# The halves of a weight chunk word by word in one buffer: a two-layer fp32 network on one core

## The reference

```python
def _conv_ffn(h, w_in, conv_w, conv_b, w_out):
    u = h @ w_in                                   # 2048 -> 2 x 5632
    ...
    return (jax.nn.silu(gate) * val) @ w_out       # 5632 -> 2048

for i in range(DEPTH):
    a = _rmsnorm(h, norm_mix[i])
    ...                                            # y: latent or windowed attention
    h = h + y
    h = h + _conv_ffn(_rmsnorm(h, norm_ffn[i]), ...)
return _rmsnorm(h, final_norm)
```

## Time and profile before

| | us |
|---|---|
| median of 2 runs | 1994.73 |
| lowest, highest | 1994.3, 1995.16 |
| span of the profiled execution | 1992.6 |
| PE busy in it | 1979.7 (99%) |
| DVE, ACT, POOL busy | 1418.9 (71%), 992.0 (50%), 143.9 (7%) |

### The profile page before, as it was taken

The page is one execution under the profiler, slowest core; times in us unless marked ns, Lnnn a source line. Parts: engine busy times, 40 slices in busy tenths (PEclk is TensorE's granted clock), DMA queues, the critical chain, the costliest instruction groups (busy, mean ns, idle before and its releaser), DMA issues.

```text
span 1992.6 us, 33224 instructions
## 1 busy us (share of the span) xinstructions
PE 1979.7 (99%) x11726; PEld 1746.3 (88%) x11726; DVE 1418.9 (71%) x1969; ACT 992.0 (50%) x1180; POOL 143.9 (7%) x157
## 2 busy tenths in 40 slices
PE   9999999999999999999999999999999999999998
PEld 8998888888888888888899899888888888888886
DVE  6856788877887786554567668788778877865444
ACT  6556445555545554343455654554555555534433
POOL 1112220000000000110120004100000000011000
PEclk9999999999999999999999999999999999999999
DMA  8566655555555555556575445655555556676654
GB/s 299 177 196 161 196 188 189 177 200 191 189 175 193 193 194 192 190 176 205 191 237 179 132 136 179 197 184 178 190 193 195 189 183 196 207 235 213 200 188 137
DMA packets 106870, 379.67 MB, mean 191 GB/s; under 512 B 12107, under 2 KB 12684, under 8 KB 106668
## 3 DMA queue, kind: packets, MB, share of 16 engines
q1 hardware_dynamic: 102332, 362.22, 54.7%
q0 software_dynamic: 4176, 16.07, 3.2%
q10 hardware_dynamic: 288, 0.33, 0.1%
HBM read 368.09 MB, written 10.49 MB: 190 GB/s over the span
## 4 chain that ended last, share of the span: by engine, by line
PE 96%; DVE 2%; DMA 1%; SPq 0%; ACT 0%; issue 0%; ACTq 0%
PE ps L429 46%; PE ps L432 24%; PE ps L823 4%; PE ps L822 4%; PE ps L821 4%; PE ps L723 2%; PE ps L725 2%; PE ps L724 2%; DMA raw<-weights 1%; DVE w_lo L1172 1%; PE ps L761 1%; PE ps L784 1%; PE ps L459 1%; PE ps L460 1%; PE ps L458 1%; PE ps L772 1%
## 5 line engine op out<-in xcount | busy, mean ns | idle before, releaser
L1172 DVE TENSOR_TENSOR w_lo<-raw,w_hi 128x1024 fp32r<-128x1024 f32 (+1 forms) x678 | 824.9, 1230 | 498.5 <-ACT w_hi L861 477.2
L861 ACT ACTIVATE w_hi<-raw 128x1024 fp32r<-128x1024 f32 (+1 forms) x678 | 710.4, 1054 | 778.4 <-PE ps L432 454.9
L429 PE MATMUL ps<-op_in,w_hi 128*128 128x512 f32 x2992 | 1026.4, 391 | 1.7 <-DVE w_lo L1205 0.9
L432 PE MATMUL ps<-op_in,w_lo 128*128 128x256 f32 x2992 | 812.3, 282 | 0.0
L429 PEld LDWEIGHTS ps<-op_in,w_hi 128*128 128x128 f32 x2992 | 548.9, 188 | 106.1 <-issue 1.3
L432 PEld LDWEIGHTS ps<-op_in,w_lo 128*128 128x128 f32 x2992 | 564.8, 189 | 15.7
L429 PE MATMUL ps<-op_ffn,w_hi 128*128 128x512 f32 x704 | 243.1, 390 | 0.0
L432 PE MATMUL ps<-op_ffn,w_lo 128*128 128x256 f32 x704 | 195.8, 282 | 0.0
L429 PEld LDWEIGHTS ps<-op_ffn,w_hi 128*128 128x128 f32 x704 | 131.1, 188 | 26.5
L821 PE MATMUL ps<-w_hi,op_ffn 128*128 128x512 f32 x352 | 139.5, 396 | 0.0
L822 PE MATMUL ps<-w_lo,op_ffn 128*128 128x512 f32 x352 | 139.5, 396 | 0.0
(11 more groups left out here) (218 smaller groups left out, 2052.4 us busy)
## 6 DMA issues: line engine op xcount, KB each, us to landing
raw<-weights SPq DMA_DIRECT2D x662, 512.0 KB, 4.1
raw<-weights SPq DMA_DIRECT2D x16, 384.0 KB, 3.1
bias_rows<-brow POOLq DMA_DIRECT2D x1, 6144.0 KB, 36.1
win_bias<-bias_rows POOLq DMA_DIRECT2D x4, 1024.0 KB, 8.4
h<-xt SPq DMA_DIRECT2D x8, 256.0 KB, 7.2
raw<-weights SPq DMA_DIRECT2D x8, 256.0 KB, 6.2
x_tok<-x_rows SPq DMA_DIRECT2D x4, 512.0 KB, 8.7
h_rows<-h_blocks POOLq DMA_DIRECT2D x16, 128.0 KB, 5.5
```

Source lines behind the costliest of these rows:

```text
L429: return mm(ps[:, bank, 0:2 * T], whi, op, start=start, stop=stop)
L432: return mm(ps[:, bank, 0:T], wlo, op[:, 0, :], start=False, stop=False)
L861: f(w_hi[s][:, 0:cols], raw[s][:, 0:cols], ACT.Copy).then_inc(hi_ready, 1)
L1172: v.tensor_tensor(w_lo[s][:, 0:cols], raw[s][:, 0:cols], w_hi[s][:, 0:cols].bitcast(F32), ALU.subtract).then_inc(lo_ready, 1)
```

## The change

`w_hi[s]` and `w_lo[s]` are no buffers of their own any more. A slot of the ring is one buffer of 2048 words; in it a chunk's high and low half lie in one of two ways, by how PE will use the chunk:

- word by word (`w_hi`, `w_lo`: even and odd words), where all its tiles are stationary: a_in, a_q, a_out, f0_in, f0_out, the last 32 chunks of b_in, b_out, f1_in;
- one behind the other as before (`rows_hi`, `rows_lo`: first and last 1024 words), where a chunk or part of it moves: a_kv, the first 8 chunks of b_in, f1_out.

ACT and DVE write with the same choice, and DVE reads the high half with it. Since the layout is fixed when the program is built, loops are split where it changes: ACT's and DVE's loops over a_kv, over f0_out (unrolled: 88 chunks) and the last turn of f1_in. Number, size and order of matmuls, splits, loads and waits stay the same.

```diff
-    w_hi = [new(f"w_hi{s}", [P, CH], F32R) for s in range(SLOTS)]
-    w_lo = [new(f"w_lo{s}", [P, CH], F32R) for s in range(SLOTS)]
+    ring = [new(f"ring{s}", [P, 2 * CH], F32R) for s in range(SLOTS)]
+    w_hi = [r[:, :].rearrange("p (c two) -> p c two", two=2)[:, :, 0] for r in ring]
+    w_lo = [r[:, :].rearrange("p (c two) -> p c two", two=2)[:, :, 1] for r in ring]
+    rows_hi = [r[:, 0:CH] for r in ring]
+    rows_lo = [r[:, CH:2 * CH] for r in ring]
...
-            def w_chunk(n, op, kt0, first, last, b0, tiles=(0, 1, 2, 3)):
+            def w_chunk(n, op, kt0, first, last, b0, tiles=(0, 1, 2, 3), halves=(w_hi, w_lo)):
                 s = n.mod(SLOTS)
+                whi, wlo = halves[0][s], halves[1][s]
                 pe.wait_ge(lo_ready, (n + 1).v)
                 for j, m in enumerate(tiles):
                     for k in range(2):
                         c = k * COLS + m * P
-                        z = feature_tile(b0 + j, w_hi[s][:, c:c + P], w_lo[s][:, c:c + P],
+                        z = feature_tile(b0 + j, whi[:, c:c + P], wlo[:, c:c + P],
                                          op[:, kt0 + k, :, :], first and k == 0, last and k == 1)
...
-                        mm(o, hi, wcols(w_hi[s], k), start=first and k == 0, stop=False)
-                        mm(o, hi, wcols(w_lo[s], k), start=False, stop=False)
-                        z = mm(o, lo, wcols(w_hi[s], k), start=False, stop=last and k == 1)
+                        mm(o, hi, wcols(rows_hi[s], k), start=first and k == 0, stop=False)
+                        mm(o, hi, wcols(rows_lo[s], k), start=False, stop=False)
+                        z = mm(o, lo, wcols(rows_hi[s], k), start=False, stop=last and k == 1)
...
-            def split(n, cols=CH):
+            def split(n, cols=CH, hi=w_hi):
...
-                f(w_hi[s][:, 0:cols], raw[s][:, 0:cols], ACT.Copy).then_inc(hi_ready, 1)
+                f(hi[s][:, 0:cols], raw[s][:, 0:cols], ACT.Copy).then_inc(hi_ready, 1)
...
-            def split(n, cols=CH):
+            def split(n, cols=CH, halves=(w_hi, w_lo)):
...
-                v.tensor_tensor(w_lo[s][:, 0:cols], raw[s][:, 0:cols], w_hi[s][:, 0:cols].bitcast(F32),
+                v.tensor_tensor(halves[1][s][:, 0:cols], raw[s][:, 0:cols], halves[0][s][:, 0:cols].bitcast(F32),
                                 ALU.subtract).then_inc(lo_ready, 1)
...
-                repeat(act, 0, FFN_TURNS, body)
+                repeat(act, 0, FFN_TURNS - layer, body)
+                if layer == 1:
+                    body(None, FFN_TURNS - 1)
...
-            residual(PH["f0_out"], FT, OP0["f0_out"])
+            residual(PH["f0_out"], FT, OP0["f0_out"], rows_next=True)
```

More of the change, by code:

```diff
@@ L820, in rows_half @@
                     hi, lo = op_ffn[1][:, kt0 + k, 0, t], op_ffn[1][:, kt0 + k, 1, t]
-                    mm(ps[:, bank + half, :], hi, w_hi[s][:, w], start=first and k == 0, stop=False)
-                    mm(ps[:, bank + half, :], hi, w_lo[s][:, w], start=False, stop=False)
-                    z = mm(ps[:, bank + half, :], lo, w_hi[s][:, w], start=False, stop=last and k == 1)
+                    mm(ps[:, bank + half, :], hi, rows_hi[s][:, w], start=first and k == 0, stop=False)
+                    mm(ps[:, bank + half, :], hi, rows_lo[s][:, w], start=False, stop=False)
+                    z = mm(ps[:, bank + half, :], lo, rows_hi[s][:, w], start=False, stop=last and k == 1)
                 return z
@@ L954, in q_group @@
                 for c in range(2):
-                    split(k.times(2) + (ph.c0 + AHEAD_2 + c), cols)
+                    split(k.times(2) + (ph.c0 + AHEAD_2 + c), cols, w_hi if cols < CH else rows_hi)
                     if c == 0 and k.c == 5:
@@ L974, in kv_group @@
                     for c in range(2):
-                        split(k.times(2) + (ph.c0 + AHEAD_2 + c))
-            repeat(act, 0, 3, lambda i: [kv_group(Lin(k, 2, i)) for k in range(2)])
-            kv_group(Lin(6))
+                        split(k.times(2) + (ph.c0 + AHEAD_2 + c), hi=rows_hi if k.c < 5 else w_hi)
+            repeat(act, 0, 2, lambda i: [kv_group(Lin(k, 2, i)) for k in range(2)])
+            for k in range(4, 7):
+                kv_group(Lin(k))
             kv_group(Lin(7), False)
@@ L1033, in body @@
                     for j in range(2 * per):
-                        split(Lin(ph.c0 + AHEAD + j + 2 * per * t, 2 * per, i))
+                        next_rows = rows_next and t == 1 and j >= 2 * per - AHEAD
+                        split(Lin(ph.c0 + AHEAD + j + 2 * per * t, 2 * per, i), hi=rows_hi if next_rows else w_hi)
                         gi, at = divmod(j, per)
@@ L1037, in body @@
                             op_high(Lin(k0 + gi + 2 * t, 2, i), op_in[:, sl(Lin(4 * gi + 8 * t, 8, i), 4), 0, :])
-                if second:
+                if rows_next:
+                    body(None, 0)
+                if second or rows_next:
                     body(None, 1)
@@ L1141, in _ @@
                 for c in range(FT // 2):
-                    split(Lin(ph.c0 + AHEAD + FT // 2 * g + c))
+                    split(Lin(ph.c0 + AHEAD + FT // 2 * g + c), hi=rows_hi)
                     if c == 19:
@@ L1356, in q_group @@
                         rope_finish(Lin(8), 3, xr[:, 1, :], q_rope[:, UNITS_A - 1:UNITS_A, :])
-                    split(k.times(2) + (ph.c0 + AHEAD_2 + c), cols)
+                    split(k.times(2) + (ph.c0 + AHEAD_2 + c), cols, (w_hi, w_lo) if cols < CH else (rows_hi, rows_lo))
             for k in range(UNITS_A):
@@ L1375, in kv_group @@
                     for c in range(2):
-                        split(k.times(2) + (ph.c0 + AHEAD_2 + c))
-            repeat(dve, 0, 3, lambda i: [kv_group(Lin(k, 2, i)) for k in range(2)])
-            kv_group(Lin(6))
+                        split(k.times(2) + (ph.c0 + AHEAD_2 + c), halves=(rows_hi, rows_lo) if k.c < 5 else (w_hi, w_lo))
+            repeat(dve, 0, 2, lambda i: [kv_group(Lin(k, 2, i)) for k in range(2)])
+            for k in range(4, 7):
+                kv_group(Lin(k))
             kv_group(Lin(7), False)
@@ L1459, in add_residual, with residual @@
                 dve.wait_ge(banks_free, (g + 1).v)
-            def residual(ph, kts, k0, gain, bias=None, second=False):
+            def residual(ph, kts, k0, gain, bias=None, second=False, rows_next=False):
                 per = kts // 2
@@ L1466, in body @@
                     for j in range(2 * per):
-                        split(Lin(ph.c0 + AHEAD + j + 2 * per * t, 2 * per, i))
+                        next_rows = rows_next and t == 1 and j >= 2 * per - AHEAD
+                        split(Lin(ph.c0 + AHEAD + j + 2 * per * t, 2 * per, i),
+                              halves=(rows_hi, rows_lo) if next_rows else (w_hi, w_lo))
                         gi, at = divmod(j, per)
```

44 lines of the change are left out of this document (24 added, 20 removed).

## The result

The changed kernel takes 2024.73 us against 1994.73 us: 1.0151 times as long, 95% interval 1.0126 to 1.0175. It is 30 us slower, 1.5%, where 80 us less had been forecast. The interval does not reach 1.

What follows compares the result with a forecast made beforehand. PE, busy 99% of the span, was taken as the bound. Pairs (70.8 us) and narrow matmuls (8.9 us) were to save 79.7 us, splits and loops nothing: 1994.7 - 79.7 = 1915 us, range 1886 to 2078 us.

Steps and rivals of the forecast that it cites:

- What bounds the kernel: PE, busy 99% of the span: time is the number of matmuls times the step from start to start.
- The excess over the columns: F32R matmuls in feature_tile: 26.7 ns a pair and 10.0 ns a narrow matmul over their columns, put down to colliding streams.
- With a step of 8 bytes the load advances as fast as an F32R operand moves: Stepped weight loads on PE: distance between load and moving operand stays constant; at best 106 us less in all.
- three quarters of the gain: Changed pairs and narrow matmuls on PE: 17.5 ns less a pair, 6.2 a narrow one, 79.7 us in all.
- The place matters: Wide matmuls in f0_out and f1_out, same size and clock, different operands: 3.8 ns apart, so excess is no fixed price.
- Loads get slower: Rival, PE's weight loads: a tile spread over 1024 bytes doubles the excess, 106 us more, 2101 us; chance 0.11.
- The splits: ACT's copy (1059 ns) and DVE's subtraction (1232 ns) of 1024 columns keep their length with a step of two words.
- DVE's 0.57 us of room a split: In f0_in, with 176 splits, each split may grow by 0.57 us before DVE is full.
- DVE becomes the bound: Rival, f0_in and f1_in: splits grow to 2.1 us, 2080 us in all, break-even at 1.86 us; chance 0.15.
- The excess is F32R's own: Rival, F32R matmuls on PE: excess is a price of F32R itself, the step changes nothing, 1995 us; chance 0.16.
- The signs to look for: Right if f0_out pairs step by about 329 ns, narrow matmuls 110, f1_out's 234, splits 1232 and 1059, f0_in about 465 us.
- the first step: The claimed PE gain from stepped weight tiles; wrong if pairs still step by 347 ns or above.

Runs made afterwards that it cites:

- m3_columns: Kernel of its own, 24 matmuls a line averaged over eight places, varying tile size, step, moving columns and type; F32R with 512 columns 231 ns, BF16 216.
- m2_places: Kernel of its own, 16 pairs a line in feature_tile's order at 16 activation starts; mean pair 351.8 ns contiguous, 354.4 word by word.
- m1_steps: Kernel of its own, rows of equal matmuls, copies and subtractions at several steps; F32R with 512 columns 227 to 234 ns without steps, 233 or 234 at two.

## Why the prediction was wrong

**What bounds the kernel: right.** PE's step from start to start is the time; nothing that the change did to ACT's, DVE's or SP's work reached the end, though ACT's copies grew.

**The excess over the columns: read rightly, put down to the wrong thing.** The failing step is "With a step of 8 bytes the load advances as fast as an F32R operand moves", and before it the reading of the earlier trace rows on which it stood. That row has plain fp32 passes with 1.7 ns of excess beside a weight load, and I took from it that a load at the moving operand's pace does no harm. It differs from an F32R matmul in a second way, the pace of the moving operand, and the runs point to this one: in m3_columns the excess stays with a quarter of the weight columns, grows with the moving ones, and is nearly gone with 2-byte words at the same columns per period. The term "three quarters of the gain", 79.7 us, had nothing behind it: at equal paces no start that was tried came near the 320 ns of a pair's columns (the best stepped one in m2_places took 350), and in the kernel a pair's excess grew from 26.7 to 33.3 ns. I also called the row's x2 two matmuls; m3_columns shows two records for each plain fp32 matmul (48 for 24), so they were two passes of one. The 215 ns hold for a pass, but such a row could not show what a matmul at full pace does.

**The place matters: right, and underrated.** The 3.8 ns between wide matmuls of the same size pointed to it (by their own starts 228.5 in f0_out against 234.3 in f1_out, so nearly 6). But I carried over none of it to the question that decides here: how good is the place that the kernel has now, and is it as good for another pattern of reads? By the table of the four places, the step costs 12.8 us in the mean over them; the other 17 us are the place, which was 12 us better than the mean for contiguous tiles and is 5 us worse than the mean for stepped ones. Worked out from the single measurements: 2.6 ns x 4048 = 10.5 us and about 2 ns x 1440 = 3 us for the step, near the 12.8.

**Loads get slower: the right rival in its sign, far too dear.** It was priced at 106 us by doubling the excess; doubling it over the same counts (26.7 and 10.0 ns) would even be 122 us, since the 106 leave out the 1.7 ns a matmul. A load in steps of two words is 8 to 9 ns longer (197 for 188 or 189) and its turn 7 ns longer (118 for 110 to 112). This length hides beside 512 moving columns and nearly so beside 256; the 7 ns of a pair's wide matmul are not explained by it.

**The splits: right.** DVE unchanged, ACT 56 ns longer a copy by itself and 73 in the mean in the kernel, both hidden. DVE's 0.57 us of room a split was in no danger.

**DVE becomes the bound: did not occur**, since its rate holds at two words. At four words (1979 ns) it would have passed the break-even of 1.86 us that the prediction gives.

**The excess is F32R's own: nearest to the truth of the rivals.** Most of it comes with 4-byte words at full pace, whatever the load. The change did not leave it alone, though.

**The signs to look for: they worked.** A pair at 347 or above was named as what would refute the first step, and it stands at 353.3.

**The range: luck.** 2024.73 us lies between the 1886 and 2078 us of the prediction only because its upper part was kept for longer splits. These did not come, and the slower loads, the rival nearest to what came, were left out of it.

Left open: why the place matters, why it matters differently with steps, and why it is the wide matmul of a pair that pays for both and not the small one. A meeting of the streams in parts of the memory would fit the test in which only the distance of the two operands counted, but the stream of 4-byte words has its excess even beside a load of 32 columns, and no run tells what it meets there. Nor did any run show that places repeat after 128 bytes; only starts within 128 bytes were compared.

## What to carry to other kernels

When a row shows a cheap case, list every way in which it differs from the dear one before taking one of them for the cause; here two differed, and a kernel of equal matmuls settles it in one run. A change of an access pattern also changes how good the present placement is, so compare it at several starts of the operands, not at the one at which the old pattern happens to be good: 25 us lay in that number, nearly as much as in the change. When a sequence slows down, look at each matmul of it by its own start: here one of two paid for nearly everything. Where PE is busy 99% of the time and another engine has room, a longer instruction there costs nothing, and 7 ns a pair of matmuls on PE cost 1.5% of the kernel.

## What the runs showed of the hardware

- F32R with 512 moving columns steps by 231 ns in the mean over places (m3_columns, granted clock 1.00, the 2.4 GHz level), BF16 by 216; for F32R the tile's columns (128 or 32) make no difference. Over the pure 213.3 and 106.7 ns, F32R with 32 weight columns has 17.5 and 10 ns of excess, BF16 2.5 and 2.9.
- By the place of the operands alone a pair of F32R matmuls with contiguous tiles took 347 to 360 ns (m2_places) and the whole kernel 1994.73 to 2019.82 us.
- A weight load of 128 columns of 4-byte words paces PE at 110 to 112 ns without steps and 118 at two words (m3_columns, 128 moving columns), 173 at three, 233 at four (m1_steps, 256 moving columns).
- The moving operand minds steps more: in m1_steps 256 F32R columns read in steps of two words took 3.69 us for 16 matmuls, 231 ns each, for 118 without (rows below, L163). The change kept moving weights contiguous, and rightly so.

```profile
213.78 3.87 PE L163 MATMUL ps<-M,W 128*128 128x256 f32 x16
217.47 3.92 PE L164 MATMUL ps<-M,W 128*128 128x256 f32 x16
```

- ACT and DVE take 2.0 us for 1024 columns at a step of four words, 1.04 and 1.22 us without steps, 1.10 and 1.22 at two words.
